# Sixteen identity matmuls in each step of a chunk recurrence on TensorE

## The chip, the cores and the metric

The kernel runs on one core of a Trainium2 chip, so there is no partner to wait for. TensorE multiplies, VectorE and ScalarE evacuate its results from PSUM, SyncE and GpSimd issue DMAs. The metric is the device time of one execution in microseconds; the time of a kernel is the median of its runs. TensorE's granted clock is shown in profiles as a share of full speed: 1.00 is 2.4 GHz, 0.50 is 1.2 GHz.

## The reference

One inference step through two layers of a decoder, for a prompt of 256 tokens and 8 sample rows of 8 tokens. The even layer is attention with a dense feed-forward, the odd layer has an RWKV-7 mixer (8 heads of 64), a retention mixer and a mixture of experts. The part that matters here is the RWKV-7 recurrence of the odd layer, from a state `s` of 64x64 for each head:

```python
def rwkv7_scan(r, w, k, v, kk, a, s0):
    def step(s, inp):
        r_t, w_t, k_t, v_t, kk_t, a_t = inp
        sa = jnp.einsum('bhvk,bhk->bhv', s, -kk_t)
        s = (s * w_t[:, :, None, :] + sa[..., None] * (kk_t * a_t)[:, :, None, :]
             + v_t[..., None] * k_t[:, :, None, :])
        return s, jnp.einsum('bhvk,bhk->bhv', s, r_t)
```

Everything is float32. The outputs are the activations of both groups and the new states and caches.

## The kernel before, in words

The program is a row of phases (setup, projection, attention, dense feed-forward, retention, RWKV preparation, the RWKV recurrence, its output, experts). Behind each phase stands a barrier of all engines, so a phase begins when the last engine has finished the one before. A few weight loads are issued early in a phase; in the recurrence phase nothing of a later phase is loaded.

`rwkv_chunks_phase` (L1441) computes the recurrence in chunks of 32 tokens: 8 chunks of the prompt, which depend on each other through the state, and 8 samples with one chunk each. `STEPS` is 8, and each step takes one prompt chunk (u = 0) and one sample (u = 1), with PSUM banks 0 to 3 for u = 0 and 4 to 7 for u = 1. Every stage works on 8 heads. TensorE's order of work is written out in the loop at L1549: chunk_a for u = 0 and u = 1, then chunk_b for both, chunk_c for both, chunk_d for both, then the next step. In the text a0 is chunk_a of u = 0, a1 that of u = 1, and so on.

- chunk_a (L1497 to L1510): the chunk's own products (L1504, contraction over 64 rows), transposes of keys (L1507) and a copy of the values through the identity matrix (L1509), both on 128 rows. It needs the state of the step before (`ev_s`, `ev_y`). VectorE then masks and copies into GE, BKN and VV (L1596 to L1600).
- chunk_b (L1512 to L1523): right-hand sides, L1518 (32 rows) and L1521 (64 rows). It waits for VectorE's four copies (`ev_a`). ScalarE copies the result into RH (L1568), VectorE adds to it (L1624).
- chunk_c (L1525 to L1533): the solve with a matrix inverted beforehand, L1532 (32 rows). It waits for RH (`ev_b`), in the first step also for the inverse to come back by DMA (`moved`). ScalarE copies the result into VV (L1571).
- chunk_d (L1535 to L1546): output and state update, L1543 to L1545 (64 rows). It waits for VV (`ev_c`). VectorE updates the state ST_c (L1628, L1630) and adds into YT (L1633), ScalarE copies into YT (L1575).

PSUM bank 4u + 1 holds half of the products of chunk_a and chunk_b. The semaphore that chunk_c waits for says that VectorE has read it, and the next to write it is chunk_a of the next step. chunk_a of the first step, and VectorE's copies for it, are done ahead of the loop on VectorE, which then inverts the matrices (about 48 us, in which TensorE waits in the first chunk_c). Behind the loop TensorE turns the states back (L1560), they are stored, and the phase ends.

A matmul call on float32 data leaves two records of loading and two of multiplying in the trace, a transpose one.

Of the kernel before, what the change touches and what calls it, by code (L numbers as in the profile page):

```python
# [12 lines left out]
P = 128  # L13
# [71 lines left out]
def hybrid_step(nc, io, stop=None):  # L85
# [4 lines left out]
    def sb(name, shape, dt=F32):  # L90
        return stage[-1].enter_context(nc.sbuf_tensor(name, shape, dt))
# [13 lines left out]
    PS = root.enter_context(nc.psum_tensor("PS", [P, 8, 512], F32))  # L105
# [7 lines left out]
    ident = sb("ident", [P, P])  # L113
# [1327 lines left out]
    def rwkv_chunks_phase(AR, BK, VS, PEND, YT):  # L1441
# [15 lines left out]
        def lo(h):  # L1457
            return slice(64 * (h % 2), 64 * (h % 2) + 64)

        with nc.Block() as block:  # L1460
            @block.sync
            def _(sp):
                for b in range(NB):
                    sp.dma_start(SN[:, b], io["state_rwkv"][b].rearrange("(i g) v k -> (g v) i k", g=2)).then_inc(loaded, 16)
                sp.dma_start(GM[:], io["chunk_mask"]).then_inc(loaded, 16)

                sp.wait_ge(m_out, 8)
                sp.dma_start(scratch_u.rearrange("q s t -> s q t"), UU[:]).then_inc(moved, 16)
                sp.wait_ge(moved, 16)
                sp.dma_start(UB[:], scratch_u).then_inc(moved, 16)  # L1470
                sp.wait_ge(solved, 1)
                sp.dma_start(scratch_w, WB_[:]).then_inc(moved, 16)
                sp.wait_ge(moved, 48)
                sp.dma_start(UU[:], scratch_w.rearrange("q s t -> s q t")).then_inc(moved, 16)
                sp.wait_ge(so_out, 5)
                sp.dma_start(io["rwkv_prompt"].rearrange("o (i g) v k -> (g v) (o i) k", g=2), SO[:, 0]).then_inc(stored, 16)
                sp.dma_start(io["rwkv_sample"].rearrange("b (i g) v k -> (g v) b i k", g=2), SO[:, 1:]).then_inc(stored, 16)
                sp.wait_ge(stored, 32)

            @block.tensor  # L1480
            def _(pe):
                pe.wait_ge(loaded, 16 * NB + 16)

                for n in range(8):
                    for j in range(16):
                        c, h = 4 * (n % 4) + j // 4, 2 * (j % 4) + n // 4
                        mm = pe.matmul(PS[0:CH, n, j * CH:(j + 1) * CH], BK[lo(h), h // 2, c, 0, :], AR[lo(h), h // 2, c, 0, :], start=True, stop=True)
                    mm.then_inc(m_done, 1)

                pe.wait_ge(m_out, 8)  # L1490
                for b in range(NB):
                    for h in range(NH):
                        c = (b % 2) * 256 + h // 2 * HD
                        mm = pe.matmul(PS[lo(h), b // 2, c:c + HD], SN[lo(h), b, h // 2, :], ident[lo(h), lo(h)], start=True, stop=True)
                mm.then_inc(sn_turned, 1)

                def chunk_a(s, u):  # L1497

                    c = s + 8 * u
                    if s >= 1:  # L1500
                        pe.wait_ge(ev_s[u], 3 * s)
                        pe.wait_ge(ev_y[u], s)
                    for h in range(NH):
                        pe.matmul(PS[0:64, 4 * u + h % 2, h // 2 * 64:(h // 2 + 1) * 64], BK[lo(h), h // 2, c].rearrange("p a t -> p (a t)"),  # L1504
                                  AR[lo(h), h // 2, c].rearrange("p a t -> p (a t)"), start=True, stop=True)
                    for i in range(4):
                        pe.transpose(PS[0:64, 4 * u + 2, i * P:(i + 1) * P], BK[:, i, c].rearrange("p a t -> p (a t)"), ident[:])  # L1507
                    for i in range(4):
                        mm = pe.matmul(PS[CH:2 * CH, 4 * u + 3, i * P:(i + 1) * P], VS[:, i, c, :], ident[:], start=True, stop=True)  # L1509
                    mm.then_inc(ga[u], 1)  # L1510

                def chunk_b(s, u):  # L1512

                    c = s + 8 * u
                    st = 1 + s if u else 0
                    pe.wait_ge(ev_a[u], 4 * (s + 1))
                    for h in range(NH):
                        pe.matmul(PS[0:CH, 4 * u + 3, h * 64:(h + 1) * 64], GE[CH:2 * CH, u, h, 0:CH], VV[CH:2 * CH, u, h * 64:(h + 1) * 64],  # L1518
                                  start=True, stop=True)
                    for h in range(NH):  # L1520
                        mm = pe.matmul(PS[0:CH, 4 * u + h % 2, h // 2 * 64:(h // 2 + 1) * 64], AR[lo(h), h // 2, c, 0, :],  # L1521
                                       ST[lo(h), st, h // 2, :], start=True, stop=True)
                    mm.then_inc(rb[u], 1)  # L1523

                def chunk_c(s, u):  # L1525

                    c = s + 8 * u
                    if s == 0 and u == 0:
                        pe.wait_ge(moved, 64)
                    pe.wait_ge(ev_b[u], 2 * (s + 1))  # L1530
                    for h in range(NH):
                        mm = pe.matmul(PS[0:CH, 4 * u + 2, h * 64:(h + 1) * 64], UU[:, c * NH + h, :], RH[:, u, h * 64:(h + 1) * 64], start=True, stop=True)  # L1532
                    mm.then_inc(sc[u], 1)  # L1533

                def chunk_d(s, u):  # L1535

                    c = s + 8 * u
                    st = 1 + s if u else 0
                    pe.wait_ge(ev_c[u], s + 1)
                    for h in range(NH):  # L1540
                        i = h // 2
                        new = VV[:, u, h * 64:(h + 1) * 64]
                        pe.matmul(PS[lo(h), 4 * u, i * CH:(i + 1) * CH], ST[lo(h), st, i, :], AR[lo(h), i, c, 1, :], start=True, stop=True)  # L1543
                        pe.matmul(PS[lo(h), 4 * u + 3, 256 + i * CH:256 + (i + 1) * CH], new, GE[:, u, h, CH:2 * CH], start=True, stop=True)
                        mm = pe.matmul(PS[lo(h), 4 * u + 3, i * HD:(i + 1) * HD], BKN[:, u, h * 64:(h + 1) * 64], new, start=True, stop=True)  # L1545
                    mm.then_inc(yd[u], 1)  # L1546

                pe.wait_ge(st_set, 5)
                for s in range(STEPS):  # L1549
                    for stage_of in (chunk_a, chunk_b, chunk_c, chunk_d):  # L1550
                        for u in range(2):
                            stage_of(s, u)

                for u in range(2):
                    pe.wait_ge(ev_s[u], 3 * STEPS)
                    pe.wait_ge(ev_y[u], STEPS)
                for b in range(1 + NB):
                    for h in range(NH):
                        c = (b % 2) * 256 + h // 2 * HD
                        mm = pe.matmul(PS[lo(h), b // 2, c:c + HD], ST[lo(h), b, h // 2, :], ident[lo(h), lo(h)], start=True, stop=True)  # L1560
                mm.then_inc(so_turned, 1)
# [1116 lines left out]
```

## Time and profile before

| | |
|---|---|
| median of 3 runs | 2608.74 us |
| lowest and highest | 2597.95, 2609.36 us |
| profiled execution | 2615.0 us, span 2613.2 us |
| granted TensorE clock, mean over the span | 0.88 |
| TensorE busy | 2139.9 us (82%) |
| recurrence loop, first chunk_c to L1560 | 1478 to 1617 us |

The profile is one execution of the program. Busy time is counted from the start to the end of each instruction, so a matmul at the low clock is busy for longer. The clock isn't shown for an instruction but for a stretch of time, as a mean.

### The profile page before, as it was taken

To read this page: it belongs to the slowest core of one execution; us is meant where nothing else is said; L and a number is where in the kernel's file an instruction comes from. 1 tells how busy PE (TensorE), PEld (TensorE's weight loads), DVE (VectorE), ACT (ScalarE), POOL (GpSimd) and SP (SyncE) were. 2 spreads that over 40 slices of the span, in tenths; PEclk is the share of its full clock that TensorE was granted. 3 is DMA by queue.
4 is the path that set the end of the run, shared out by engine and by line. 5 is a ranking of instruction groups with operands and counts; after the bars stand their busy time and mean duration, and the time that the engine had idled before them with its cause. 6 is when DMAs were issued, how large, how long until landed. Compare 5 with 4: busy or idle time off the path is not lost. (4 is left out here: it accounts for less than half of the span.)

```text
span 2613.2 us, 53183 instructions
## 1 busy us (share of the span) xinstructions
PE 2139.9 (82%) x22941; PEld 1432.6 (55%) x22941; DVE 639.6 (24%) x1329; ACT 352.3 (13%) x882; POOL 105.6 (4%) x182
## 2 busy tenths in 40 slices
PE   6797678778779999777864397689999999999975
PEld 2474345445357776556533387456676666667643
DVE  1203344343220000213055643331111211111103
ACT  1102323223010000002020011021011001001001
POOL 0000002112100000000010000000000000000001
PEclk8898889899889999885876566789999999999987
DMA  9417789999653230311301000186997879899895
GB/s 362 175 65 259 244 256 327 273 296 313 224 193 129 96 113 0 129 54 36 115 15 33 17 2 20 65 294 254 345 365 280 326 278 365 323 384 344 299 393 174
DMA packets 274638, 538.00 MB, mean 206 GB/s; under 512 B 32693, under 2 KB 62258, under 8 KB 274412
## 3 DMA queue, kind: packets, MB, share of 16 engines
q1 hardware_dynamic: 261238, 493.14, 54.1%
q0 software_dynamic: 12960, 41.43, 4.6%
q8 instruction: 178, 2.92, 0.5%
q14 instruction: 48, 0.39, 0.0%
q10 hardware_dynamic: 214, 0.13, 0.0%
HBM read 520.81 MB, written 13.83 MB: 205 GB/s over the span
## 5 line engine op out<-in xcount | busy, mean ns | idle before, releaser
L348 PE MATMUL PS<-H,w_ring 128*128 128x320 f32 (+1 forms) x1008 | 281.0, 442 | 55.3 <-DMA w_ring<-in_w_in_odd 24.7
L2088 PE MATMUL PS<-moe_ring,moe_X 128*32 128x256 f32 (+1 forms) x5376 | 300.0, 371 | 25.9 <-DMA moe_ring<-in_moe_w 18.8
L2108 PE MATMUL PS<-moe_ring,moe_HT 128*32 128x256 f32 x4224 | 268.6, 384 | 4.8 <-issue 3.5
L348 PEld LDWEIGHTS PS<-H,w_ring 128*128 128x128 f32 (+1 forms) x1008 | 194.7, 194 | 141.4 <-issue 30.9
L2088 PEld LDWEIGHTS PS<-moe_ring,moe_X 128*32 128x32 f32 x5376 | 180.6, 112 | 130.2 <-issue 26.0
L2088 PE MATMUL PS<-moe_ring,H 128*32 128x256 f32 (+1 forms) x3840 | 205.5, 363 | 3.6 <-issue 2.7
L1055 PE MATMUL PS<-H,ffn_ring 128*128 128x320 f32 x704 | 191.3, 435 | 15.8 <-PEq L265 15.8
L2108 PEld LDWEIGHTS PS<-moe_ring,moe_HT 128*32 128x32 f32 x4224 | 146.3, 111 | 71.0 <-issue 11.1
L750 PE MATMUL PS<-ident,KV 128*128 128x128 f32 x832 | 118.3, 303 | 80.0 <-DMA KV<-in_cache_win_kv 35.4
L1055 PEld LDWEIGHTS PS<-H,ffn_ring 128*128 128x128 f32 x704 | 134.6, 191 | 72.5 <-issue 17.2
L2088 PEld LDWEIGHTS PS<-moe_ring,H 128*32 128x32 f32 x3840 | 131.2, 111 | 67.6 <-issue 4.1
L750 PEld LDWEIGHTS PS<-ident,KV 128*128 128x128 f32 x832 | 103.6, 155 | 104.8 <-issue 51.5
L2325 DVE TENSOR_TENSOR moe_hid<-moe_silu,PS 128x128 f32<-128x128 f32 x120 | 34.5, 288 | 477.7 <-ACT moe_silu L2225 477.7
L2225 ACT ACTIVATE moe_silu<-PS 128x128 f32<-128x128 f32 (+1 forms) x144 | 38.6, 268 | 668.1 <-PE PS L2088 668.1
L1066 PE MATMUL PS<-ffn_hidden,ffn_ring 128*128 128x320 f32 x352 | 96.7, 438 | 3.7 <-issue 3.7
L834 DVE COPY KTT<-PS 128x512 f32<-128x512 f32 x104 | 71.8, 692 | 106.1 <-PE PS L750 76.8
L663 POOL DMA_DIRECT2D KV<-in_cache_moba_kv x128 | 69.8, 545 | 609.1 <-issue 344.4
L2343 DVE TENSOR_TENSOR moe_Y<-moe_Y,PS 128x256 f32<-128x256 f32 x120 | 50.5, 421 | 165.3 <-PE PS L2108 165.3
L839 ACT ACTIVATE KTT<-PS 128x512 f32<-128x512 f32 x104 | 62.1, 597 | 189.5 <-PE PS L750 189.5
L1066 PEld LDWEIGHTS PS<-ffn_hidden,ffn_ring 128*128 128x128 f32 x352 | 67.7, 193 | 32.5 <-issue 5.2
L145 PE MATMUL PS<-ada_ring,CT 128*32 128x512 f32 x384 | 57.3, 727 | 21.9 <-DMA ada_ring<-in_ada_w 21.1
L2117 PE MATMUL PS<-moe_SL,HN 128*128 128x96 f32 (+3 forms) x336 | 73.4, 356 | 1.0 <-DVE moe_SL L2356 1.0
(452 smaller groups left out, 2081.2 us busy)
## 6 DMA issues: line engine op xcount, KB each, us to landing
moe_ring<-in_moe_w SPq DMA_DIRECT2D x168, 1024.0 KB, 11.1
moe_ring<-in_moe_w SPq DMA_DIRECT2D x40, 2048.0 KB, 16.6
ada_ring<-in_ada_w SPq DMA_DIRECT2D x24, 2048.0 KB, 18.2
KV<-in_cache_win_kv SPq DMA_DIRECT2D x128, 256.0 KB, 9.0
KV<-in_cache_moba_kv POOLq DMA_DIRECT2D x128, 256.0 KB, 6.2
KV<-in_cache_moba_kv SPq DMA_DIRECT2D x128, 256.0 KB, 7.7
ffn_ring<-in_ffn_w SPq DMA_DIRECT2D x14, 2048.0 KB, 15.9
moe_ring<-in_moe_w SPq DMA_DIRECT2D x32, 512.0 KB, 9.4
```

The costliest lines, as they stand in the source:

```text
L145: last = pe.matmul(PS[32 * j:32 * j + 32, banks[n % len(banks)], :], CT[:, 2 * j + a, :], self.RING[:, n % self.R, 2 * j + a, :], start=(a ...
L348: last = pe.matmul(PS[0:width, g % B, 0:TOK], RING[:, n % R, k, m:m + width], rhs[:, k, :], start=(k == 0), stop=(k == KT - 1))
L663: eng.dma_start(KV[:, slot, x, :], pool[bass.ds(page, 1), kv].rearrange("o p n -> (o p) n")).then_inc(chunk_in[1 + odd][slot], 16)
L750: tr = pe.transpose(PS[:, KBANK[t % 3], i * P:(i + 1) * P], KV[:, slot, x, i * P:(i + 1) * P], ident[:])
L834: copy(KTT[:, chunk % 2, s, :, x * P:(x + 1) * P], PS[:, KBANK[t % 3], :].rearrange("p (i n) -> p i n", n=P)).then_inc(done, 1)
L839: return act.activation(out, in_, ACT.Copy)
L1055: mm = pe.matmul(PS[:, 2 * (f % 2) + w, 0:TOK], RING[:, (n + w) % R, k, m * P:(m + 1) * P], rhs[:, k, :], start=(k == 0), stop=(k == KT - 1))
L1066: mm = pe.matmul(PS[:, 4 + o, 0:TOK], RING[:, n % R, k, o * P:(o + 1) * P], HT[:, k0 + k, :], start=(k0 + k == 0), stop=(k0 + k == FT - 1))
L2088: mm = pe.matmul(PS[32 * j:32 * j + 32, i % 2, 0:2 * w].rearrange("p (a n) -> p a n", a=2), X[:, k, UNIT * u:UNIT * (u + 1)], RING[:, slot ...
L2108: mm = pe.matmul(PS[32 * g:32 * g + 32, 3, 0:256], HT[:, i % 2, 32 * j:32 * j + 32], rows[:, 256 * g:256 * (g + 1)], start=(j == 0), stop= ...
L2117: mm = pe.matmul(PS[:, 4 + k // per, k % per * (512 // per):k % per * (512 // per) + n], HN[0:rows, t, k * P:(k + 1) * P], SL[0:rows, buf, ...
L2343: last = dve.tensor_tensor(Y[:, buf, u, :], Y[:, buf, u, :], part, ALU.add)
```

## The change

Four matmuls of the identity matrix with itself, 128x128 each, are written side by side over the whole of bank 4u + 1, behind each chunk_c and behind each chunk_d. That is 16 in a step and 128 in all. Nothing reads what they write, they wait for nothing and signal nothing: the increment of a stage stands on its own last matmul, ahead of them.

```diff
+                def stay_busy(u):
+
+                    for part in range(4):
+                        pe.matmul(PS[:, 4 * u + 1, part * P:(part + 1) * P], ident[:], ident[:], start=True, stop=True)
+
                 def chunk_a(s, u):
...
                     for h in range(NH):
                         mm = pe.matmul(PS[0:CH, 4 * u + 2, h * 64:(h + 1) * 64], UU[:, c * NH + h, :], RH[:, u, h * 64:(h + 1) * 64], start=True, stop=True)
                     mm.then_inc(sc[u], 1)
+                    stay_busy(u)
...
                         mm = pe.matmul(PS[lo(h), 4 * u + 3, i * HD:(i + 1) * HD], BKN[:, u, h * 64:(h + 1) * 64], new, start=True, stop=True)
                     mm.then_inc(yd[u], 1)
+                    stay_busy(u)
```

## Rows read from the trace of the kernel before

**Rows 1.** Page, busy time (1: us, share, instructions); chain of waits, first piece that it reaches

```profile
PE 2139.9 (82%) x22941; PEld 1432.6 (55%) x22941; DVE 639.6 (24%) x1329; ACT 352.3 (13%) x882; POOL 105.6 (4%) x182
...
1704.30 0.02 issue
```

**Rows 2.** Stretches, one for each of seven steps of the recurrence, and their sum

```profile
core 0: us, PE busy (x) PEld busy (x) DVE busy (x) ACT busy (x) POOL busy (x), PEclk, DMA share, GB/s
1481.50:1500.30 18.80, 17.77 (x249) 15.25 (x248) 7.53 (x18) 2.82 (x6) 0.00 (x0) 0.68 0.01 2
...
1518.60:1536.35 17.75, 17.24 (x250) 15.26 (x249) 7.53 (x18) 2.82 (x6) 0.00 (x0) 0.69 0.01 2
...
sum 129.00, PE 122.88 PEld 105.92 DVE 52.72 ACT 19.73 POOL 0.00; mean PE 17.55 PEld 15.13 DVE 7.53 ACT 2.82 POOL 0.00
```

**Rows 3.** Stretches of one us inside the first steps, same columns

```profile
1483.00:1484.00 1.00, 1.00 (x24) 1.00 (x23) 0.00 (x0) 0.00 (x0) 0.00 (x0) 0.50 0.00 0
...
1492.00:1493.00 1.00, 1.00 (x9) 0.80 (x8) 0.67 (x1) 0.00 (x0) 0.00 (x0) 0.96 0.06 16
...
1498.00:1499.00 1.00, 0.55 (x9) 0.38 (x7) 0.61 (x2) 0.59 (x1) 0.00 (x0) 0.95 0.00 0
...
1515.00:1516.00 1.00, 1.00 (x25) 0.91 (x20) 0.05 (x1) 0.59 (x1) 0.00 (x0) 0.98 0.00 0
...
1533.00:1534.00 1.00, 1.00 (x12) 1.00 (x12) 0.37 (x2) 0.59 (x1) 0.00 (x0) 0.52 0.00 0
```

**Rows 4.** Waits of TensorE, 1481 to 1620: us in total, times, longest

```profile
PE PS L1518 <- DVE VV L1600: 3.9, 7, 0.6
PE PS L1532 <- DVE RH L1624: 2.3, 6, 0.5
```

**Rows 5.** Timeline, TensorE, first step: start us, us, instruction [idle before]

```profile
1477.96 3.62 PE L1532 MATMUL PS<-RH,UU 32*32 32x64 f32 x32 [48.32 <-DMA UU<-scratch_w]
...
1481.51 0.28 PEld L1543 LDWEIGHTS PS<-AR,ST_c 64*64 64x64 f32 x2 [0.17 <-issue]
...
1486.44 0.36 PE L1504 MATMUL PS<-AR,BK 64*64 64x64 f32 x1
...
1488.66 1.92 PE L1509 MATMUL PS<-ident,VS 128*32 128x128 f32 x8
...
1490.51 1.12 PE L1504 MATMUL PS<-AR,BK 64*64 64x64 f32 x16
...
1492.34 1.06 PE L1509 MATMUL PS<-ident,VS 128*32 128x128 f32 x8
...
1493.33 1.08 PE L1518 MATMUL PS<-VV,GE 32*32 32x64 f32 x16
...
1495.56 1.08 PE L1518 MATMUL PS<-VV,GE 32*32 32x64 f32 x16 [0.58 <-DVE VV L1600]
...
1497.13 1.07 PE L1532 MATMUL PS<-RH,UU 32*32 32x64 f32 x16
...
1498.66 1.73 PE L1532 MATMUL PS<-RH,UU 32*32 32x64 f32 x16 [0.46 <-DVE RH L1624]
```

**Rows 6.** Timeline, TensorE, a full stationary tile in the sample attention

```profile
316.28 3.64 PE L750 MATMUL PS<-ident,KV 128*128 128x128 f32 x16 [12.98 <-DMA KV<-in_cache_win_kv]
...
369.95 4.01 PE L750 MATMUL PS<-ident,KV 128*128 128x128 f32 x32
```

**Rows 7.** Timeline, TensorE, chunk_a of first and second step; turning the states back

```profile
1421.45 0.68 PE L1504 MATMUL PS<-AR,BK 64*64 64x64 f32 x16 [2.59 <-DVE ST_c L1590]
...
1425.84 1.07 PE L1518 MATMUL PS<-VV,GE 32*32 32x64 f32 x16
...
1505.49 1.06 PE L1504 MATMUL PS<-AR,BK 64*64 64x64 f32 x14
...
1511.48 1.08 PE L1518 MATMUL PS<-VV,GE 32*32 32x64 f32 x16
...
1617.22 6.46 PE L1560 MATMUL PS<-ident,ST_c 64*64 64x64 f32 x144 [1.29 <-DVE YT L1633]
```

## The prediction

> **What bounds the kernel now.** I read the page first: TensorE is busy for 82% of the span, so it is the first suspect everywhere, but that is an average over stages [rows 1]. The chain of waits doesn't reach the place of the change: it begins at 1704 us, behind the barrier that closes each phase [rows 1]. The recurrence stands at 1478 to 1617 us, between two barriers, so what it gains or loses moves everything behind it by as much; nothing behind it starts earlier, and it has almost no DMA to collide with (DMA share 0.01). So I read this stage by itself.
>
> The table of stretches, one for each step, shows TensorE busy 122.88 of 129.00 us, VectorE 52.72, ScalarE 19.73, and a granted clock of 0.68 to 0.69 [rows 2]. Steps last 17.75 to 18.80 us, 18.43 in the mean. The clock is the point: of its two levels, 1.2 GHz (0.50) and 2.4 GHz (1.00), the stage has the low one nearly two thirds of the time, though TensorE is almost never idle. The single microseconds show when [rows 3]: low through all of chunk_d (TensorE busy 1.00 at clock 0.50), still low in the first half of chunk_a, high from 1492 us on, behind the matmuls on 128 rows (L1507, L1509), and low again at 1498.9, 1516.0 and 1533.0, each time in chunk_c, behind the narrow matmuls of chunk_b and chunk_c (32 and 64 rows) with their waits. So a busy column doesn't hold the clock; what runs in it does.
>
> The waits that TensorE has here are few: 3.9 us for VV before the second chunk_b, 2.3 us for RH before the second chunk_c [rows 4], and 1.29 us before L1560 [rows 7]. There is little idle time in which sixteen more matmuls could hide.
>
> **The change, part by part.** It adds one thing: four full matmuls behind each of the two chunk_c and two chunk_d of a step, 8 steps. A matmul call in fp32 leaves two records in the trace (L1509: 4 calls, 8 records), so a filler group is 8 records of 128 rows by 128 moving columns, four groups a step, 32 groups in all. It waits on nothing, signals nothing (the increments stand on the real matmul before it), and only what is queued behind it on TensorE is late. VectorE and ScalarE get their semaphores as before. No DMA is touched.
>
> Price of a group. L1509 has this very shape but for a narrower stationary tile: 8 records from 1488.66 to 1490.51, 1.85 us at the low clock, and 1492.34 to 1493.33, 0.99 us at the high one [rows 5]. The full 128x128 stationary tile costs no more: L750 runs 16 records in 3.64 us at the low clock and 32 in 4.01 us at the high one, 1.8 and 1.0 us for eight [rows 6]. So 59.2 us if all 32 are slow, 31.7 us if all are fast.
>
> What hides of it. (a) The wait of the second chunk_c for RH: with c0 as 0.95 us of matmuls, c1 begins 1.53 us after c0 (1497.13 to 1498.66), 0.46 of it idle; some 0.5 us of cover in steps 2 to 8 [rows 4, 5]: 3.5 us. (b) The last filler lies beside VectorE's work before L1560: 1.3 us [rows 7]. Together 4.8 us. The 0.17 us before chunk_d has no engine as its releaser, so I leave it. The fillers behind chunk_d hide nothing of their own: chunk_a begins right behind them now (1486.44), its semaphores long set [rows 5]. The waits of chunk_b stay: they hang on VectorE's copies behind L1509, and no filler stands there.
>
> What the clock gives back. Chunk_a of both groups runs from about 1486.6 to 1493.33 in the first step and 1505.4 to 1511.48 in the second; all at the high clock it takes 1421.45 to 1425.84, 4.39 us [rows 5, 7]. I take 6.2 us as the present mean, so a chunk_a wholly at the high clock gives 1.8 us; seven steps follow a chunk_d with fillers: 12.6 us. L1560 behind the last filler (6.46 us now, partly slow) gives about 1.0 us [rows 7]. The fourth group of a step then lies across the rise and costs the mean, 1.42 us, the first three 1.85 each.
>
> Why the first three slow: the fall comes in the stretch of b0, b1 and c0, and the first filler stands behind that stretch. Nothing in the change touches what TensorE does before that. The clock then has to be won back by fillers mixed with chunk_c (32 rows) and chunk_d (64 rows), which themselves hold it down; the filler rows are of the kind that ran before the rises. I expect the rise around the second chunk_d or the filler behind it, sooner than now by a microsecond or several.
>
> Sum: 8 x (3 x 1.85 + 1.42) = 55.8; less cover 4.8; less clock 12.6 + 1.0. **Net +37.4 us.** The profiled execution took 2615.0 us around its span of 2613.2, 6.3 above the median of the three runs, 2608.74. So +37 gives 2652 for an execution like it, and a median of 2608.7 + 37.4 = **2646 us**.
>
> A rule speaks the other way. The Trainium skill (TensorE: Matmul & The Clock Gate, section Why this matters for your kernels) advises to keep TensorE busy without gaps so that it keeps 2.4 GHz; read simply, the fillers close the gaps and the clock stays up. The trace agrees in part: the clock does fall where there are waits, but it also stays low with a busy share of 1.00 in chunk_d [rows 3]. By the rule the result would be that of rival 1.
>
> **Rivals.** 1. *The clock stays at 2.4 GHz from step to step.* For it: in the first chunk_b it was still high, and fillers behind c0 and c1 might come just in time. Price of a step, all fast: chunk_a 4.39; b0 with the wait to b1 2.2; b1 1.57; c0 and c1 with fillers 2 x 1.94; chunk_d (5.1 us for both now, 1481.51 to about 1486.6) at the ratio of L1504 (1.12 us slow, 0.68 fast) 3.1; its fillers 2 x 0.99 = 2.0: together 17.1 us against 18.43 [rows 5, 7]. Seven steps give 9 us; the first fillers, which begin at the low clock after 48 us of waiting for a DMA, cost 5 us of it back [rows 5]; the end gives 3. So -7 us: 2602. It decides from the point where the clock is still high when the filler behind c0 starts, in nearly every step. For it too: the fall at 1498.9 came when a filler behind c0 would have been running. Against it: at 1516.0 it came while c0 still ran (b0 at 1511.48, plus 2.2 and 1.57, puts c0 at 1515.2), and what goes before c0 is unchanged [rows 3, 7]. As no row shows chunk_d at 2.4 GHz, its 3.1 us lies between 2.55 (half) and 5.1.
>
> 2. *The fillers don't raise the clock any earlier.* Then nothing comes back: 59.2 - 4.8 = +54: 2663. For it: chunk_d and chunk_c between the fillers are what the clock stays low in. Against: the last filler and L1504, L1507, L1509 make an unbroken run on wide rows.
>
> 3. *Some steps stay fast, some fall.* Steps have no fixed place against the moments at which the clock changes (the fall is at different places of chunk_c from step to step), so a few may slip through: with a third to half of the steps as in rival 1, +5 to +20: about 2621.
>
> 4. *Nothing is added in effect* (all hidden): 2609. TensorE's idle time in seven steps is 6.1 of 129.00 us, so there is no room for it.
>
> **How the numbers follow.** Forecast (falls in each step, won back around the last filler) 0.60, with +20 to +50; rival 2 0.17; rival 3 0.12; rival 1 0.10; rival 4 0.01. The range takes the forecast and rival 2 whole and most of rival 3: +4 to +57, 2613 to 2666. About 0.5% (13 us) is what a measurement of this kernel tells from no change. Slower by more: 0.60 + 0.17 and half of rival 3, 0.83. Within: the other half of rival 3, most of rival 1, and rival 4, 0.14. Faster by more than 13 us is only an all-fast stage with a cheaper chunk_d than I took: 0.03.
>
> **What would show it.** In the profile after: 256 more matmul records with `ident` on both sides, pitch about 0.21 us slow and 0.11 fast; seven steps of 22 to 25 us, and granted clock around 0.6 to 0.75; falls still within b1 to the first filler; chunk_a nearly all at 1.00, 4.4 to 5 us long; the wait for RH gone from TensorE's list, the one for VV unchanged at 3.9 us; the DMA-bound and later phases the same length. I am wrong if steps are near 17 us with clock 1.00 (rival 1), or if chunk_a still begins low in each step (rival 2), or if a filler group costs much more than 1.85 us, as it would if loading the full stationary tile behind narrow matmuls were not hidden.

## The result, and the profile after

The changed kernel takes 2675.84 us (median of 4 runs, 2666.34 to 2678.75), the kernel before 2606.98 us (4 runs, 2597.95 to 2609.36). The ratio is 1.026, with a 95% interval of 1.024 to 1.029: 69 us slower, where 2646 (at most 2666) was forecast. The direction was right, the size was not.

The page of the changed kernel, its span and its first row:

```profile
span 2676.9 us, 53695 instructions
...
PE 2207.5 (82%) x23197; PEld 1506.7 (56%) x23197; DVE 639.5 (24%) x1329; ACT 352.2 (13%) x882; POOL 105.5 (4%) x182
```

TensorE's 256 new records are there (23197 against 22941 matmuls, [rows 1]) and its share of busy time is the same 82%. The span grew by 63.7 us; the other 5 us of the median are the scatter of the runs. Nearly all of the 63.7 lies in the loop. From the first L1532 to L1560 the kernel before takes 139.3 us (1477.96 to 1617.22, [rows 5, 7]); after, L1537 and L1567 are the same lines, and it takes 201.8 us (1478.85 to 1680.64): +62.5. From the output phase to the end both take the same within 1.5 us. This length, from the first chunk_c to the turning of the states, is what I compare below. It is free of what varies in the rest of the kernel.

Three of the seven steps and the sum of all (columns as in [rows 2]; the last stretch of the sum ends at 1670.0, 1.1 us before its step does):

```profile
core 0: us, PE busy (x) PEld busy (x) DVE busy (x) ACT busy (x) POOL busy (x), PEclk, DMA share, GB/s
1486.50:1512.90 26.40, 25.88 (x282) 22.60 (x281) 7.53 (x18) 2.82 (x6) 0.00 (x0) 0.63 0.01 1
...
1539.30:1565.70 26.40, 25.88 (x282) 22.31 (x281) 7.53 (x18) 2.82 (x6) 0.00 (x0) 0.63 0.01 1
...
1592.00:1618.30 26.30, 25.79 (x281) 22.58 (x280) 7.53 (x18) 2.82 (x6) 0.00 (x0) 0.63 0.01 1
...
sum 183.50, PE 179.88 PEld 157.20 DVE 52.71 ACT 19.73 POOL 0.00; mean PE 25.70 PEld 22.46 DVE 7.53 ACT 2.82 POOL 0.00
```

Every step takes 26.3 to 26.4 us, against 17.75 to 18.80. The mean clock of a step fell to 0.63. VectorE and ScalarE do what they did (52.71 and 19.73 us in seven steps).

TensorE in one step, and the end of the loop (timeline). L1500 is the filler, L1509 to L1514 chunk_a, L1523 and L1526 chunk_b, L1537 chunk_c; the many short rows of chunk_d are left out:

```profile
1489.32 2.08 PE L1500 MATMUL PS<-ident 128*128 128x128 f32 x8
...
1494.11 2.07 PE L1500 MATMUL PS<-ident 128*128 128x128 f32 x8
1496.11 1.12 PE L1509 MATMUL PS<-AR,BK 64*64 64x64 f32 x16
1497.16 1.01 PE L1512 MATMUL PS<-ident,BK 128*64 128x128 f32 x4
...
1501.32 1.07 PE L1523 MATMUL PS<-VV,GE 32*32 32x64 f32 x16
...
1503.48 1.07 PE L1523 MATMUL PS<-VV,GE 32*32 32x64 f32 x16 [0.52 <-DVE VV L1607]
...
1505.21 1.91 PE L1537 MATMUL PS<-RH,UU 32*32 32x64 f32 x16
1507.05 2.08 PE L1500 MATMUL PS<-ident 128*128 128x128 f32 x8
1509.05 1.91 PE L1537 MATMUL PS<-RH,UU 32*32 32x64 f32 x16
...
1678.64 2.07 PE L1500 MATMUL PS<-ident 128*128 128x128 f32 x8
1680.64 5.16 PE L1567 MATMUL PS<-ident,ST_c 64*64 64x64 f32 x144
```

Stretches of the same step:

```profile
1486.00:1496.00 10.00, 10.00 (x115) 9.20 (x114) 2.00 (x6) 0.47 (x2) 0.00 (x0) 0.50 0.00 0
...
1497.00:1498.00 1.00, 1.00 (x10) 0.58 (x6) 0.00 (x0) 0.00 (x0) 0.00 (x0) 0.50 0.07 16
1498.00:1504.00 6.00, 5.48 (x79) 4.40 (x78) 4.43 (x10) 0.59 (x1) 0.00 (x0) 1.00 0.00 0
1504.00:1505.00 1.00, 1.00 (x26) 0.91 (x24) 0.37 (x2) 0.00 (x0) 0.00 (x0) 0.92 0.00 0
1505.00:1512.00 7.00, 7.00 (x51) 6.26 (x48) 0.74 (x2) 1.76 (x3) 0.00 (x0) 0.50 0.01 2
```

And all that TensorE waits for from 1486 us to the end of the loop (us in total, times, longest):

```profile
PE PS L1523 <- DVE VV L1607: 3.6, 7, 0.5
```

What to see there: ten microseconds of fillers and chunk_d on end, TensorE busy 10.00 of 10.00, and the clock at 1.2 GHz throughout. It comes up inside chunk_a (at 1498.0), as before, and is gone by 1505, in chunk_b, before the first filler starts. So all four groups of the step run at the low clock. It is so in all seven steps: the clock falls three times in the second chunk_b and four times in the first chunk_c, always ahead of the filler. It comes up 0.7 to 3.8 us into chunk_a, 2.3 in the mean, against 2.4 to 5.7 (4.3 in the mean) before. A group takes 2.00 us (1507.05 to 1509.05). The wait for RH has gone from the list, the wait for VV is as it was (3.6 us, [rows 4] 3.9).

### The profile page after: what moved, and what is told of

Same layout as the page of the kernel before. It is cut to its first block and busy times, and to the rows that moved or that the text cites. A ratio compares the mean times of both kernels' runs of the same rounds, so it can differ in the third digit from the quotient of the medians.

```text
span 2676.9 us, 53695 instructions
## 1 busy us (share of the span) xinstructions
PE 2207.5 (82%) x23197; PEld 1506.7 (56%) x23197; DVE 639.5 (24%) x1329; ACT 352.2 (13%) x882; POOL 105.5 (4%) x182
## 5 line engine op out<-in xcount | busy, mean ns | idle before, releaser
L750 PE MATMUL PS<-ident,KV 128*128 128x128 f32 x832 | 118.3, 303 | 78.8 <-DMA KV<-in_cache_win_kv 28.0
L2095 PEld LDWEIGHTS PS<-moe_ring,H 128*32 128x32 f32 x3840 | 142.1, 111 | 57.3 <-issue 4.1
L750 PEld LDWEIGHTS PS<-ident,KV 128*128 128x128 f32 x832 | 103.6, 156 | 103.8 <-issue 54.3
## 6 DMA issues: line engine op xcount, KB each, us to landing
moe_ring<-in_moe_w SPq DMA_DIRECT2D x40, 2048.0 KB, 16.5
```

The lines of the kernel that those rows point to most:

```text
L750: tr = pe.transpose(PS[:, KBANK[t % 3], i * P:(i + 1) * P], KV[:, slot, x, i * P:(i + 1) * P], ident[:])
L2095: mm = pe.matmul(PS[32 * j:32 * j + 32, i % 2, 0:2 * w].rearrange("p (a n) -> p a n", a=2), X[:, k, UNIT * u:UNIT * (u + 1)], RING[:, slot ...
```

## The experiments

All lengths of the loop are measured as above (before 139.3 us, changed kernel 201.8). Edits are against the changed kernel where nothing else is said. Theory A: the fillers are TensorE time at the low clock, because between chunk_c and chunk_d they are too thin to bring the clock up. Its rivals are named where they are tested. The two variants for which a ratio is given were run four times, the others once, so the comparison rests on the loop in one profile of each. The changed kernel and two variants of it that differ only in what a group is made of agree in it to 0.1 us (201.8 each).

**Half of the fillers.** Only behind chunk_c:

```diff
                     mm.then_inc(yd[u], 1)
-                    stay_busy(u)
```

> Fillers behind chunk_c alone, 16 of the 32 groups. Theory A (a group is 2.00 us of TensorE at the low clock plus some 0.16 us for the narrow matmuls behind it, less 0.5 us of cover for each step, and the clock comes up no earlier): a step of 18.43 + 2 x 2.0 + 0.2 - 0.5 = 22.1 us, total about +27 us. Rival B (the cost is the clock, which falls earlier or rises later because of the fillers; the groups themselves hide): clearly less than half of the whole change, under +15. Rival D (the groups behind chunk_c hold the clock up through chunk_d): steps of 19 us, about +5 to +10.

Measured: loop 162.1 us, +22.8; five of the seven steps take 21.8 to 21.9 us, as theory A says, the two others 19.7 and 18.5. Three steps in its stretches:

```profile
1483.50:1505.40 21.90, 21.32 (x265) 18.52 (x264) 7.53 (x18) 2.82 (x6) 0.00 (x0) 0.66 0.01 1
...
1527.30:1547.05 19.75, 19.17 (x265) 16.55 (x264) 7.53 (x18) 2.82 (x6) 0.00 (x0) 0.74 0.01 2
1547.05:1565.55 18.50, 17.98 (x265) 15.77 (x264) 7.53 (x18) 2.82 (x6) 0.00 (x0) 0.80 0.01 2
```

The two short steps have the higher clock, at the same work: here the clock stayed up once from one chunk_a to the next chunk_c, as rival D has it for every step. So the same fillers are dear or nearly free by the clock alone. Rival B (the groups hide, the clock costs) asked for less than 15 us and is out.

Only behind chunk_d:

```diff
                     mm.then_inc(sc[u], 1)
-                    stay_busy(u)
```

> Fillers behind chunk_d alone, 16 of the 32 groups. Theory A: a step of 18.43 + 2 x 2.0 + 0.2 = 22.6 us if chunk_a is left as it was, less about 1 us if the last group, which joins chunk_a's wide rows, brings the rise forward: 21.5 to 22.6 us, total +25 to +33 us. Rival B: under +15. With e1_c_only it should add up to about +65 if the parts don't act on each other.

Measured: loop 168.7 us, +29.5, all steps 22.1 to 22.4 us, as theory A has it. All seven steps:

```profile
1476.10:1631.70 155.60, 151.99 (x1850) 133.67 (x1849) 52.73 (x126) 19.73 (x42) 0.00 (x0) 0.65 0.01 2
```

The last group does bring the rise forward: chunk_a takes 5.2 us in the mean of the steps, against 6.3 before (and 5.7 to 6.6 in six of the seven steps with fillers behind chunk_c alone). The halves sum to +52.3, the whole is +62.5. Of the 10.2 us between them, 5.6 lie in the two steps of the first half that kept the clock for longer; the other 4.6, about 0.7 us in each step, no run takes apart.

**Twice the filler.**

```diff
-                    for part in range(4):
-                        pe.matmul(PS[:, 4 * u + 1, part * P:(part + 1) * P], ident[:], ident[:], start=True, stop=True)
+                    for part in range(8):
+                        pe.matmul(PS[:, 4 * u + 1, part % 4 * P:(part % 4 + 1) * P], ident[:], ident[:], start=True, stop=True)
```

> Eight matmuls for each filler instead of four (a group of 16 records). Rival C (identity matmuls don't lift the clock, or only chunk_a does): every group costs 3.7 us, steps of 26.4 + 4 x 1.7 = 33 us, total about +120 us against before. Theory A with dilution (the groups do lift the clock, but four matmuls were too few against the narrow ones around them): the clock comes up within chunk_c or chunk_d, steps of 23 to 27 us with mean clock above 0.8, total between +30 and +70 us: no more than the single filler for twice its work.

Measured: loop 168.5 us, +29.3: 256 matmuls cost half of what 128 do. Two steps of it:

```profile
1476.20:1497.40 21.20, 20.68 (x313) 18.45 (x312) 7.53 (x18) 2.82 (x6) 0.00 (x0) 1.00 0.01 2
1497.40:1520.20 22.80, 22.28 (x313) 19.94 (x312) 7.53 (x18) 2.82 (x6) 0.00 (x0) 0.93 0.00 1
```

Four of the seven steps are like the first row, with the clock at 2.4 GHz from end to end; in the three like the second it falls at about the end of c0 and is back behind the filler that follows. Rival C is refuted: identity matmuls do lift the clock, and mostly hold it. Four in a group were too few here, eight are enough. The steps, 21.2 to 22.8 us, are even shorter than the 23 to 27 expected.

**What is multiplied.** Live activations for the identity:

```diff
-    ..., ident[:], ident[:], start=True, stop=True)
+    ..., X[:, 0, 0:P], X[:, 1, 0:P], start=True, stop=True)
```

> As the changed kernel, with live activations (two 128x128 tiles of X) in place of the identity on both sides. If what TensorE multiplies doesn't matter (only that rows of the array are fed): steps of 26.3 us and mean clock 0.63 as in the changed kernel, total +60 to +72 us. If the zeros of the identity keep the clock from rising: the clock rises behind the first groups, steps under 24 us, total under +45 us.

Measured: loop 201.8 us, the very length of the changed kernel. All seven steps (1483.5 to 1668.0):

```profile
1483.50:1668.00 184.50, 180.87 (x1961) 157.80 (x1960) 52.72 (x126) 19.76 (x42) 0.00 (x0) 0.63 0.01 1
```

So the zeros of the identity did not keep the clock low.

**Twice the filler on a quarter of the rows and columns.** Eight matmuls with `PS[0:32, ...]`, `ident[0:32, 0:32]` and `ident[0:32, :]` in the place of the full ones:

> As e3_double, eight matmuls for each filler with the same 128 moving columns, but on 32 rows and 32 columns of the array instead of 128. Theory A (the clock rises with the rows fed, not with busy time): it stays low through chunk_c and chunk_d, each group costs about 3.5 us, steps of 31 to 33 us, mean clock 0.55 to 0.62, total about +100 to +120 us, for the same number of matmuls that gave steps of 21.9 us at clock 0.98 on 128 rows. Rival E (amount of matmuls alone counts): steps of 21 to 23 us, total about +28 us.

Measured: loop 247.2 us, +107.9; the total was 2720.1 us. One step, and one group of 16 records:

```profile
1485.00:1516.95 31.95, 31.37 (x314) 25.65 (x313) 7.53 (x18) 2.82 (x6) 0.00 (x0) 0.61 0.01 1
```

```profile
1487.79 3.62 PE L1500 MATMUL PS<-ident 32*32 32x128 f32 x16
```

Busy 31.37 of 31.95 us, and the clock is at 0.61. The same count of matmuls with the same moving columns, at the same places, on the full array gave 1.00 or 0.93. This is the plainest result of the study: the busy time of TensorE doesn't tell its clock, and the same matmuls on a small part of the array don't lift it. The edit cuts the rows and the stationary columns together, so by itself it doesn't say which of the two counts. The kernel before points at the rows: its clock also comes up at 1720.8 us, while L1754 multiplies on 128 rows with a stationary tile 8 columns wide (behind 6.5 us in which TensorE is idle; in the chain of waits):

```profile
1715.93 6.84 PE PS L1754 x16
```

**Five matmuls instead of four** (`range(5)`, the bank's part taken modulo 4):

> Five matmuls for each filler instead of four. If a group is just a price: 4 x 0.43 us more in each step, 28.0 us, total +82 us. If four was just short of what lifts the clock among chunk_c and chunk_d (twice as many did lift it): some steps come up early, steps between 20 and 26 us, mean clock over 0.66, total +25 to +60 us, less than with four.

Measured: loop 201.8 us, steps of 28.1, 22.6, 28.0, 28.1, 22.6, 28.0 and 25.4. Four of them:

```profile
1471.30:1499.40 28.10, 27.59 (x290) 24.32 (x289) 7.53 (x18) 2.82 (x6) 0.00 (x0) 0.62 0.01 1
1499.40:1522.00 22.60, 22.08 (x290) 19.50 (x289) 7.53 (x18) 2.82 (x6) 0.00 (x0) 0.80 0.01 1
...
1578.10:1600.70 22.60, 22.08 (x290) 19.50 (x289) 7.53 (x18) 2.82 (x6) 0.00 (x0) 0.80 0.01 1
...
1628.70:1654.10 25.40, 24.88 (x290) 21.97 (x289) 7.53 (x18) 2.82 (x6) 0.00 (x0) 0.70 0.01 1
```

The expectation of a smaller cost than with four was missed in the loop, which is equal (the total of the one run, 2661.6 us, is 51 above the kernel before, but that run was 15 us ahead of it when the loop began). But the fifth matmul is not just a price, which would have been 14 us more. In two steps the clock came up early and the step fell below the 26.4 us of the changed kernel, in a third by 1 us. So four were just short of it here, as theory A has it, but the edge is not a sharp one.

**One matmul of 512 columns** for four of 128 (`ident[:].unsqueeze(1).broadcast_to([P, 4, P])` as moving operand):

> The changed kernel's fillers as one matmul of 512 moving columns instead of four of 128: the same columns, a quarter of the stationary loads. If a group costs 2.00 us instead of the 1.85 forecast because of the one load that nothing covers at its start: still 2.0 us, steps of 26.4 us. If each load costs its share: 1.8 us or less, and steps of 25.6 us or less, with the clock up earlier in some of them.

Measured: loop 201.8 us, steps of 26.3 to 26.4. A group of one call (2 records):

```profile
1488.40 2.07 PE L1499 MATMUL PS<-ident 128*128 128x512 f32 x2
```

2.0 us to the next instruction again. So the stationary loads inside a group are hidden. What is not is the first one: in the changed kernel the first record of a group stands 0.37 us before the second, the others 0.21.

**Fillers where the clock is lost.** Two matmuls behind chunk_b and two behind chunk_c, both of u = 0, and none elsewhere. In bank 2, which VectorE has read by then, and in bank 1. The edit is against the kernel before:

```diff
+                def stay_busy(bank):
+                    for part in range(2):
+                        pe.matmul(PS[:, bank, part * P:(part + 1) * P], ident[:], ident[:], start=True, stop=True)
...
                     mm.then_inc(rb[u], 1)
+                    if u == 0:
+                        stay_busy(2)
...
                     mm.then_inc(sc[u], 1)
+                    if u == 0:
+                        stay_busy(1)
```

> Two matmuls (4 records) behind chunk_b of u = 0 and two behind chunk_c of u = 0, where TensorE waits for VectorE anyhow, and none elsewhere: 32 matmuls instead of 128, in the stretch before the clock falls. If what the clock falls on is the run of narrow matmuls and waits in chunk_b and chunk_c: the fall doesn't come, chunk_c and chunk_d run at 2.4 GHz, steps of about 14.2 to 15.5 us, total -20 to -33 us against before. If the clock falls whatever stands there: the groups lie mostly in the waits (0.58 and 0.46 us idle for about 0.5 us of work each at the high clock), steps of 18.4 to 18.9 us, total 0 to +4 us.

Measured: 2576.05 us (median of 4 runs), ratio to the kernel before 0.988, 95% interval 0.985 to 0.991: **1.2% less time than the kernel before, well clear of the scatter.** The loop takes 109.4 us, 29.9 less than before. The first step, the second and the last of its stretches:

```profile
1476.40:1494.70 18.30, 18.30 (x258) 15.70 (x257) 7.53 (x18) 2.82 (x6) 0.00 (x0) 0.71 0.01 2
1494.70:1508.35 13.65, 13.65 (x258) 11.87 (x257) 7.53 (x18) 2.82 (x6) 0.00 (x0) 1.00 0.01 2
...
1562.95:1576.60 13.65, 13.65 (x258) 11.88 (x256) 7.53 (x18) 2.82 (x6) 0.00 (x0) 1.00 0.01 2
```

And a whole step without chunk_d (L1500 the fillers, L1539 chunk_c):

```profile
1497.52 0.68 PE L1509 MATMUL PS<-AR,BK 64*64 64x64 f32 x16
...
1501.90 1.08 PE L1523 MATMUL PS<-VV,GE 32*32 32x64 f32 x16
1502.90 0.64 PE L1526 MATMUL PS<-ST_c,AR 64*32 64x64 f32 x16
1503.47 0.71 PE L1500 MATMUL PS<-ident 128*128 128x128 f32 x4
1504.11 1.08 PE L1523 MATMUL PS<-VV,GE 32*32 32x64 f32 x16
...
1505.69 1.08 PE L1539 MATMUL PS<-RH,UU 32*32 32x64 f32 x16
1506.69 0.71 PE L1500 MATMUL PS<-ident 128*128 128x128 f32 x4
1507.33 1.08 PE L1539 MATMUL PS<-RH,UU 32*32 32x64 f32 x16
```

From the second step on the clock never falls and TensorE has no idle time: the fillers (0.64 us each) stand where it waited 0.58 and 0.46 us [rows 5]. chunk_c and chunk_d at 2.4 GHz then pay: both chunk_d together take 2.84 us (1494.68 to 1497.52) against 5.1.

Is that the filled wait or the clock? The same edit on 32 rows and columns, `ident[0:32, 0:32]` and `ident[0:32, :]` into `PS[0:32, ...]`:

> e7_b0_c0 with the same matmuls at the same places, on 32 rows and 32 columns of the array instead of 128. If the clock is held by the rows fed: it falls as before, steps of 18 to 19 us, clock 0.66 to 0.70, loop within 4 us of before. If it is held by there being no idle time on TensorE: steps of 13.7 us as in e7_b0_c0, the loop 30 us shorter.

Measured: loop 131.1 us, 8.2 less than before; the total was 2595.3 us. All seven steps:

```profile
1471.36:1592.30 120.94, 120.81 (x1793) 103.00 (x1792) 52.70 (x126) 19.73 (x42) 0.00 (x0) 0.75 0.01 2
```

TensorE is busy for 120.81 of 120.94 us, as full as in the kernel above, and the clock is at 0.75, falling in every step. So 22 of the 30 us hang on the size of the fillers (128 rows and columns against 32), not on the filled waits. I expected the loop to stay within 4 us of before; that was missed, for even the narrow fillers moved the fall somewhat later.

Only the filler behind chunk_b, then only that behind chunk_c:

> e7_b0_c0 with the two matmuls behind chunk_b of u = 0 alone. If one such place is enough to hold the clock: steps of 13.5 to 14 us as in e7_b0_c0. If both are needed: the clock still falls in some or all steps, in chunk_c, steps of 15 to 17.5 us, mean clock 0.7 to 0.85, loop 10 to 20 us shorter than before.

> e7_b0_c0 with the two matmuls behind chunk_c of u = 0 alone. If the first place is the one that matters: steps of about 18 us, as before. If either place holds the clock when the fall would come there: a mixture of steps of 13.5 us and of 16 to 18 us, the loop between 5 us longer and 30 us shorter than before.

Measured: behind chunk_b alone the loop takes 131.1 us, steps of 16.5 to 18.8, mean clock 0.75. The clock falls in every step, in chunk_c or in chunk_d, and the wait for RH is there in full:

```profile
1472.55:1594.60 122.05, 118.87 (x1765) 101.73 (x1764) 52.72 (x126) 19.77 (x42) 0.00 (x0) 0.75 0.01 2
...
PE PS L1539 <- DVE RH L1631: 3.2, 7, 0.5
```

Behind chunk_c alone it takes 114.5 us (total 2575.1, one run). Two steps are as before, then the clock holds for the five that follow:

```profile
1488.55:1506.85 18.30, 17.72 (x253) 15.21 (x253) 7.53 (x18) 2.82 (x6) 0.00 (x0) 0.71 0.01 2
1506.85:1520.45 13.60, 13.08 (x254) 11.36 (x252) 7.53 (x18) 2.82 (x6) 0.00 (x0) 1.00 0.01 2
```

So the place behind c0 does most of it, and once the clock had come up in the second step it held it alone, at 13.6 us a step, although TensorE still waits 0.52 us for VV in each of them. With both places it held from one step earlier, which one profile of each can't put down to the filler behind b0. The totals of the two kernels are not to be told apart by one run.

**The first step as well.** The kernel with both, and 28 more identity matmuls in the wait for the inverted matrices (`pe.wait_ge(solved, 1)` and the fillers ahead of `pe.wait_ge(moved, 64)`; the edit is against the kernel before):

> e7_b0_c0, and 28 matmuls more in the wait of about 8 us for the inverted matrices ahead of the first chunk_c, where TensorE is idle. In e7_b0_c0 the first step was still slow (18.25 us against 13.66). If the clock comes up in that wait and holds: the first step takes 13.7 us, total -34 to -38 us against before. If the fillers end too early or too late and the clock is low again by then: the first step 18.3 us or the first chunk_c up to 3 us late, total -25 to -30 us.

Measured: 2578.35 us, ratio 0.987 (0.983 to 0.992), loop 108.7 us: nothing gained that can be measured. A slow step and the third:

```profile
1473.94:1490.62 16.68, 16.68 (x258) 14.48 (x256) 7.53 (x18) 2.82 (x6) 0.00 (x0) 0.80 0.01 2
...
1507.30:1520.95 13.65, 13.65 (x258) 11.88 (x256) 7.53 (x18) 2.82 (x6) 0.00 (x0) 1.00 0.01 2
```

The clock was up for the first chunk_c and fell in the first chunk_d; two steps of 16.7 us took the place of one of 18.3 and one of 13.7. That is nearest to the second outcome of the expectation, with the total 32.4 us below the kernel before, between the two ranges. The 28 matmuls end at 1471.3, and the matrices had arrived at 1470.7: the first chunk_c was 0.6 us late, which the length of the loop doesn't show.

## Why the forecast was wrong, point by point

- **That TensorE has no room for the fillers, that nothing behind the stage reacts, that no other engine is late:** right. TensorE is busy for 179.88 of 183.50 us, VectorE and ScalarE do the same work, and the later phases agree within 1.5 us.
- **Which rival:** it went nearly as rival 2, the fillers bring the clock up no earlier. I gave that 0.17, and priced it at +54. In full it holds for chunk_c, chunk_d and all four groups. In chunk_a the rise came some 2 us earlier than before, which gave half of the gain forecast there.
- **The step that failed: "I expect the rise around the second chunk_d or the filler behind it".** The rise came inside chunk_a, in all steps. This cost 4.6 us, as the fourth groups took 2.0 us instead of 1.42, and half of the gain in chunk_a: it takes 5.2 us in the step shown (1496.11 to 1501.32) and 5.4 in the mean of the seven, not 4.39. Against 6.3 before that is -6.2 us instead of -12.6. In three steps the clock was then gone already in the second chunk_b: +1.2 us, less 0.2 for shorter waits for VV. The kind of run that I took for enough (fillers between chunk_d) is enough with eight matmuls and, at times, with five.
- **The price of a group, 1.85 us:** 2.00 at the low clock. I read it from L1509, whose stationary tile is 32 columns wide and whose neighbours are wide already, and from the pace inside a long run of L750. The full load at the start of each group isn't in either row. 24 groups x 0.15 = 3.6 us.
- **What a filler does to its neighbour:** the sum put it at nothing, without a reason. Behind a filler a chunk_d takes 2.78 us (1491.33 to 1494.11 in the timeline), so 5.56 for both against 5.1: 8 x 0.46 = 3.7 us.
- **The cover of the wait for RH, 3.5 us:** none. The wait went, but as the clock is now low for c0 in most steps, c0 itself takes 1.65 us in the mean (0.95 at the high clock). From c0 to the filler it takes a little longer than from c0 to c1 before (1.65 against 1.53): +0.8 us instead of -3.5, and c1, now slow in every step, +0.6. The 3.5 us were also more than the 2.3 us of waits that [rows 4] have.
- **The last filler beside VectorE's work:** 1.6 us hidden, forecast 1.3. L1567 took 5.16 instead of 6.46 us, 1.3 against a forecast of 1.0.

Together: 32 x 2.00 = 64.1, plus 3.7, 0.8, 0.6 and 1.2, less 0.2, 6.2 and 1.6, is 62.4 us for a loop that grew by 62.5. The forecast for the loop was 38.4 on the same terms. Of the missing 24 us, 12 are the clock that came up too late and fell too soon (4.6 + 6.4 + 1.0), 7.3 the price of a group and of its neighbour, 4.9 the cover and c1.

The prediction also read the clock in chunk_a as low in its first half. In the kernel before it is low for 5.4 of the 6.7 us of the first step and for 4.3 of 6.3 in the mean.

By the rule of the Trainium skill named in the prediction (TensorE: Matmul & The Clock Gate, section Why this matters for your kernels) a TensorE without gaps would have kept 2.4 GHz. The measurements decide otherwise where most of the matmuls are narrow: 120.81 of 120.94 us busy at a clock of 0.75 with the narrow fillers, and 10.00 of 10.00 at 0.50 in chunk_d with groups of four. With wide matmuls in the gaps the rule holds: 13.65 of 13.65 at 1.00.

Rival 1 named the point that decides, the clock when the filler behind c0 starts. Moving the fillers there turned the change into a gain of 30 us. It priced both chunk_d at the high clock at 3.1 us. They take 2.84 with no filler between them and 3.1 (twice 1.57) with eight matmuls behind each.

What stays open: why the fall comes in some steps and not in others of the same kernel (fillers behind chunk_c alone, e1_c_only; five matmuls, e6_five; the first two steps with the filler behind c0 alone, e10_c0_only; the first two with the first step filled as well, e8_b0_c0_early). The steps differ only in when they begin against the moments at which the clock changes; I didn't vary that by itself. This limits what is said of the place, too. e1_c_only has twice as many matmuls at the place behind c0 that held the clock in e10_c0_only, and as many behind c1, and yet it lost the clock in six of seven steps. And the steps that hold it are equal in length to 0.01 us within each kernel (13.65 or 13.60 us), so a step of this length may happen to fit those moments, a rival that no run excludes. Against it stands only that the kernel with both places gained in all four of its runs, and that the clock came up at different points ahead of the held steps: 5.3 us into chunk_a there, 3.4 us in e8_b0_c0_early.

## What to carry to other kernels

A dense TensorE with a low granted clock is a stage to look at microsecond by microsecond: find where the clock is lost, and try a few full 128x128 matmuls in the waits there, not where the engine is already busy. Price a filler with the switch on both sides of it, and by a row that stands between the same neighbours. And if a filler does not change the clock, it is paid in full at the slow rate, so a forecast that leans on the clock needs the case without it as its main term, not as a rival.

## What the runs showed of the hardware

- A stage can be busy on TensorE for at least 99.9% of its time at a granted clock of 0.75 (32x32 fillers) and at 1.00 (128x128 fillers), with the same number of matmuls.
- Twice the fillers cost less: 32 groups of four +62.5 us, of eight +29.3 us. At the high clock eight matmuls of 128x128 take 1.98 us and a chunk_d behind a filler 1.57, at the low one four take 2.00 and the chunk_d 2.78.
- The first full stationary load behind narrow matmuls isn't hidden (0.37 us to the next record instead of 0.21 at the low clock), and at the low clock one matmul of 512 columns takes as long as four of 128.
- Operands of zeros and ones or live data: the same clock, the same loop to 0.1 us.
